# One program for a pooling block, an attention block and a mixture of experts: new starting stage, new opening of the experts, new ending

## What is computed

```python
def first_block(x, ...):
    for layer in range(2):
        h = rms_norm(x, mix_pre_g[layer])
        if layer < 1:
            m = pool_mixer(h, pool_w[layer], pool_scale[layer])
        else:
            m = stick_breaking_attention(h @ w_q, k, v) @ w_o
        x = x + rms_norm(m, mix_post_g[layer])
        h = rms_norm(x, mlp_pre_g[layer])
        x = x + rms_norm(square(relu(h @ w_up)) @ w_down, mlp_post_g[layer])
...
def pool_mixer(h, w_grp, scale):      # windows 2, 4, 8, 16, one for each 256 channels
    ...                               # mean of the last w tokens, minus the token itself
    y = einsum('bsgc,gcd->bsgd', y, w_grp).reshape(B, S, D)
    return y * scale
...
def hierarchical_moe(h, ...):         # 4 groups of 8 experts, two experts for a token
    act = silu(h @ w_gate) * (h @ w_up) * comb
    y = y + act @ w_down              # then h + y
```

## Time and profile before

| | us |
|---|---|
| median of three runs | 1147.08 |
| the profiled execution | 1151.92 |
| its span in the trace | 1150.1 |
| first product of the first up projection | 41.6 |
| first products of the experts (gather) | 703.0 |
| last chunk there, its products begin | 1138.1 |

### The profile page before, as it was taken

How to read it: one execution, slowest core, us unless ns; L and a number is a source line. 1 busy time by engine, 2 the same in 40 slices (tenths; PEclk the granted TensorE clock), 3 DMA queues, 4 the chain that set the end, 5 groups by cost and what they waited for, 6 DMA issues and landing times.

```text
span 1150.1 us, 14626 instructions
## 1 busy us (share of the span) xinstructions
PE 953.5 (83%) x5897; PEld 713.3 (62%) x5897; DVE 483.6 (42%) x798; ACT 384.0 (33%) x687; POOL 1.9 (0%) x7
## 2 busy tenths in 40 slices
PE   5899999999998999999799888967675656566666
PEld 4789998879866998998688776424141423232231
DVE  3655565665456566556766763220101010101010
ACT  3554554564475455455555532100000000000000
POOL 0000000000000000000000000000000000000000
PEclk9899999999999999999899998988887878888879
DMA  9545455544305354545440688999999999999995
GB/s 355 207 156 211 152 213 182 183 165 157 137 2 178 132 198 172 213 151 215 147 142 6 249 325 329 427 427 427 428 429 428 427 429 429 429 429 427 427 422 234
DMA packets 62738, 310.44 MB, mean 270 GB/s; under 512 B 2529, under 2 KB 3553, under 8 KB 52321
## 3 DMA queue, kind: packets, MB, share of 16 engines
q1 hardware_dynamic: 62256, 308.17, 67.7%
q0 software_dynamic: 432, 1.57, 0.5%
HBM read 308.68 MB, written 1.05 MB: 269 GB/s over the span
## 4 chain that ended last, share of the span: by engine, by line
PE 69%; DMA 17%; DVE 8%; ACT 4%; issue 2%; SPq 1%; DVEq 0%
DMA ring<-in_w_exp_down 17%; PE ps L636 15%; PE ps L637 14%; PE ps L638 14%; PE ps L1073 6%; PE ps L1117 6%; PE ps L1057 5%; PE ps L1129 3%; DVE w_lo L1655 1%; PE ps L827 1%; SPq L595 1%; DVE hT_lo L1636 1%; ACT w_hi L1238 1%; PE ps L701 1%; ACT hT_hi L1208 1%
## 5 line engine op out<-in xcount | busy, mean ns | idle before, releaser
L1642 DVE TENSOR_TENSOR w_lo<-ring,w_hi 128x1024 fp32r<-128x1024 f32 x158 | 190.7, 1223 | 84.7 <-ACT w_hi L1223 84.7
L1223 ACT ACTIVATE w_hi<-ring 128x1024 fp32r<-128x1024 f32 x158 | 164.5, 1054 | 88.3 <-PE ps L638 82.2
L1073 PE MATMUL ps<-ring,x 128*32 128x512 f32 x992 | 128.8, 677 | 78.6 <-DMA ring<-in_w_exp_up 67.3
L636 PE MATMUL ps<-hT_hi,w_hi 128*128 128x256 f32 x656 | 188.0, 287 | 4.5 <-DVE hT_lo L1636 2.7
L637 PE MATMUL ps<-hT_lo,w_hi 128*128 128x256 f32 x656 | 186.8, 285 | 0.0
L638 PE MATMUL ps<-hT_hi,w_lo 128*128 128x256 f32 x656 | 186.8, 285 | 0.0
L1073 PEld LDWEIGHTS ps<-ring,x 128*32 128x32 f32 x992 | 37.7, 123 | 163.4 <-issue 160.7
L636 PEld LDWEIGHTS ps<-hT_hi,w_hi 128*128 128x128 f32 x656 | 127.1, 194 | 6.4 <-issue 5.0
L637 PEld LDWEIGHTS ps<-hT_lo,w_hi 128*128 128x128 f32 x656 | 127.2, 194 | 0.5
L638 PEld LDWEIGHTS ps<-hT_hi,w_lo 128*128 128x128 f32 x656 | 127.0, 194 | 0.0
L1117 PE MATMUL ps<-ring,moe 128*32 128x512 f32 x512 | 69.3, 701 | 56.4 <-DMA ring<-in_w_exp_down 55.0
(11 more groups left out here) (280 smaller groups left out, 1176.6 us busy)
## 6 DMA issues: line engine op xcount, KB each, us to landing
ring<-in_w_exp_down SPq DMA_DIRECT2D x32, 2048.0 KB, 19.7
ring<-in_w_exp_gate SPq DMA_DIRECT2D x31, 2048.0 KB, 19.4
ring<-in_w_exp_up SPq DMA_DIRECT2D x31, 2048.0 KB, 20.4
ring<-in_w_up SPq DMA_DIRECT2D x16, 2048.0 KB, 8.1
ring<-in_w_down SPq DMA_DIRECT2D x16, 2048.0 KB, 7.8
ring<-in_w_in SPq DMA_DIRECT2D x6, 2048.0 KB, 8.5
ring<-in_w_kv SPq DMA_DIRECT2D x4, 2048.0 KB, 10.3
ring<-in_w_q SPq DMA_DIRECT2D x2, 2048.0 KB, 9.7
```

The lines of the kernel that those rows point to most:

```text
L636: mm(out, a_hi, b_hi, start=start, stop=False, skip_group_check=True)
L1073: last = mm(wk(side)[q, :], xgT[:, k, q], w4[:, j, k % 2, :] if opening else w[j][:, k, :], start=(k == 0), stop=(k == KD - 1))
L1223: fn(parts(n if edge else None, f)[0].rearrange("p (k w) -> p k w", k=KD), src, ACT.Copy).then_inc(hi_ready, 1)
L1642: ve.tensor_tensor(lo, src, hi.bitcast(F32), ALU.subtract).then_inc(lo_ready, 1)
```

## The change

**Start.** `x` comes in two transfers with a semaphore each, and the norm, `h`, the pooling and the mixer's own norm are done for one half at a time. `poolm` holds only what isn't zero: 144 columns (BAND) for half 0, 128 for half 1. `packed` is in two: its first 56 columns early, the rest now behind `consts`. The transfers keep their order. PE first writes zeros into banks 4 to 7 (16 products), and the pooling adds to them. `scale_row` is multiplied into `pool_w` on DVE (`pool_scaled`), in two parts, instead of into the result. ACT takes pooled groups 0 to 5, DVE 6 and 7; line 711's successor waits group by group. The squares are taken from `acc` in halves of 512 channels by ACT while DVE multiplies the other half by `row`. The splits of the first `w_up` chunk stand behind the mixer: quarter 0 between the token halves, 1 to 3 behind both. `keep_busy` is 8 ahead of the second half's transposes instead of 14 ahead of the first's.

```diff
+            for s in range(TT):
+                sp.dma_start(x[:, s, :], a["x"][0, s * P:(s + 1) * P, :]).then_inc(x_loaded[s], 16)
+            sp.dma_start(kbuf[:, 0:pool_ends[-1]], a["poolm"]).then_inc(poolm_loaded, 16)
+            sp.dma_start(packed[:, 0:S_QKG], a["packed"][:, 0:S_QKG]).then_inc(packed_loaded, 16)
...
-            sp.dma_start(row[:, :], a["mix_post_g"][0].partition_broadcast(P)).then_inc(scale_loaded, 16)
+            sp.dma_start(row[:, :], a["mix_post_g"][0].partition_broadcast(P)).then_inc(gain_loaded, 16)
+            load(N_MLP[0], kd_rows(a["w_up"][0])[:, :, 0:COLS], KD, COLS)
+            sp.dma_start(consts[:, :], a["consts"]).then_inc(consts_loaded, 16)
+            sp.dma_start(packed[:, S_QKG:], a["packed"][:, S_QKG:]).then_inc(packed_rest_loaded, 16)
...
+            pe.wait_ge(zero_ready, 1)
+            for b in range(4):
+                keep_busy(4 + b, 4)
             pe.wait_ge(poolm_loaded, 16)
+            pe.wait_ge(h_ready, 1)
+            for k in range(KD):
+                mm(wk(k // 2)[:, (k % 2) * T:(k % 2) * T + BAND], h[:, 0, k * P:(k + 1) * P], poolm[0][:, k // 2, :],
+                   start=False, stop=False, skip_group_check=True)
...
                 for g in range(4):
+                    if s == 0:
+                        pe.wait_ge(pool_scaled, g // 2 + 1)
+                        pe.wait_ge(yT_lo, g + 1) if g < 3 else pe.wait_ge(yT_hi, 1)
...
-                    if s == layer:
-                        keep_busy(7, (14, 10)[layer])
+                    if s == 1:
+                        keep_busy(7, (8, 10)[layer])
...
+            mix_half(0)
+            root(0, mix_ms, 1, mix_r0)
+            mix_half(1)
+            act.wait_ge(consts_loaded, 16)
+            root(1, mix_ms, 2, mix_r0)
             take_half(0, 0, 0, 0)
-            for f in (2, 3):
+            split(1, 0, quarter(1, 0))
+            take_half(0, 1, 2, 0)
+            for f in (1, 2, 3):
                 split(1, f, quarter(1, f))
```

and on DVE:

```diff
+            for part in range(2):
+                w = slot(N_POOL)[:, 1024 * part:1024 * part + 1024].rearrange("p (g c d) -> p g c d", g=2, c=2)
+                scales = scale_row[:, 512 * part:512 * part + 512].rearrange("p (g d) -> p g d", g=2)
+                ve.tensor_tensor(w, w, scales.unsqueeze(2).to_broadcast([P, 2, 2, 256]), ALU.mult).then_inc(pool_scaled, 1)
...
+            def mix_half(s):
+
+                dve.wait_ge(quarters_used, 2 * s + 2)
+                for half in (1, 0):
+                    if half == 0:
+                        dve.wait_ge(mix_squares, 2 * s + 1)
+                    c = slice(half * COLS, (half + 1) * COLS)
+                    ve.tensor_tensor(mg[:, s, c], acc[:, s, c], row[:, c], ALU.mult).then_inc(mix_gained, 1)
...
             for s in range(TT):
+                mix_half(s)
+                mix_add(s)
```

```diff
+            seed(0, 0)
+            turn_half(x, 1, x_ready, 10, 6)
             router(0)
-            turn_half(x, 1, x_ready, 10, 6)
             router(1)
...
+            seed(0, 1)
+            keep_busy(7, 7)
+
             pe.wait_ge(ind_ready, 1)
...
+                    for pair in range(4):
+                        gather(pair)
+                        if pair < 2:
+                            seed(1, pair)
+                        elif pair == 3:
+                            turn_weights()
+                        pe.wait_ge((xg_lo, xg_hi)[pair // 2], pair % 2 + 1)
+                        project_slots(0, (2 * pair, 2 * pair + 1), None)
```

```diff
+                            if closing and c == CPB - 1:
+
+                                sp.dma_start(dst[:, :, 0:COLS], src[:, :, 0:COLS]).then_inc(loaded, 16)
+                                sp.dma_start(dst[:, :, COLS:], src[:, :, COLS:]).then_inc(tail_loaded, 16)
+                                continue
...
+                        if closing and f == 3 and half == 1:
+                            pe.wait_ge(tail_loaded, 16)
...
+                        if closing:
+                            last.then_inc(moe_done, 1)
...
+            for half in range(2):
+                act.wait_ge(moe_done, 2 * half + 1)
+                leave(half)
             with act.If(n_most > SLOTS):
```

235 lines of the change are left out of this document (126 added, 109 removed).

## The result

| | us |
|---|---|
| the changed kernel, median of four runs | 1136.18 (1135.7 to 1138.89) |
| the kernel before, median of four runs beside it | 1147.15 |
| ratio | 0.990, 95% interval 0.9886 to 0.9914 |
| the profiled execution of the changed kernel, and its span | 1138.89, 1137.1 |
| the forecast | 1128.4 (1123.5 to 1133.5) |

Faster by 11 us, and 7.8 us short of the forecast; two more jobs with the unedited changed kernel gave 1134.82 and 1134.85, 13.0 under the kernel before of the same jobs. The direction and most mechanisms were right, the size and the range were not.

A forecast was written before the change was run, and what follows sets the result against it. TensorE's order of work was taken to bound the kernel up to the router, then the stream of experts' weights. Start -15.1, opening -0.7 and ending -2.9 sum to -18.7: 1147.08 to 1128.4 us, range 1123.5 to 1133.5.

The forecast's parts named there:

- start and both blocks: Start up to the experts: -15.1 us from an earlier up projection and full clock; feed-forward 1, attention and second block unchanged.
- opening: Opening of the experts: fewer seeds ahead of the gather free chunk 0 earlier; -0.7 us, with low clock in the gather +1.5.
- tail: Ending: half the last products remain and only the last store's issue follows its copy; -2.9 us, -3.6 if the branch is free.
- The start's step of 12.1 us: First mixer done by halves: TensorE starts the up projection at 29.5 instead of 41.63, 12.1 us earlier.
- Quarter 1's thin cover: First up projection: the split of quarter 1 comes at 31.7, TensorE wants it at 32.4; cover 0.7 us thin.
- The clock term of 3.0 us: First up projection: the clock stays up where 6.13 us ran at 0.50; 3.0 us more, bounds 0 and 3.1.
- rival 1: Clock falls in the start or one more place later: 6.13 us at half speed stay, +3.0, 1131.4; chance 0.15.
- Falls further on: Short clock falls behind the start may land elsewhere when everything comes earlier; taken as 0, with 3 us either way.
- a second hole: Opening: the stream gets a second hole of 2.4 us ahead of load 13, which can only flow at 725.2.
- rival 4: Opening: copies and waits of the pairs run the stream dry longer, low clock in the gather; +2.2, 1130.6; chance 0.09.
- a second transfer's fixed time: Ending, last chunk in two loads: no gap between transfers taken; about 2.0 us each in series would leave -0.9, whole 1130.4.
- rivals 1 to 4: Beside rivals 1 and 4: late loads (`scale_row` at 13.4), 1130.8, chance 0.09; fewer clock falls further on, 1125.4, chance 0.10.

The follow-up runs named there:

- consts_first: Changed kernel with the 532 KB of consts issued ahead of the pooling matrix's weights, scale row and first up chunk instead of behind them; 1136.92 us.
- before_again: The kernel before, unedited, profiled a second time; 1148.67 us, ratio 1.0006.
- before_busy: The kernel before with 5 more zero products ahead of the first transposes and 10 more behind them; 1147.94 us, ratio 1.0000.
- end: The kernel before with only the ending's part of the change (last chunk in two loads, quarters copied and stored singly); 1145.84 us, ratio 0.9983.
- after_third: The changed kernel, unedited, measured again in a third job; 1134.85 us, ratio 0.9879.
- start: The kernel before with only the start part of the change (loads and first mixer); 1137.2 us, ratio 0.9924.
- kb18: The changed kernel with 18 instead of 7 zero products between the second seed and the counting of the tokens; 1133.53 us, ratio 0.9875.
- kb18_again: The changed kernel with 18 instead of 7 zero products ahead of the counting, a second time; 1133.76 us, ratio 0.9866.
- after_again: The changed kernel, unedited, measured again beside its own variants; 1134.82 us, ratio 0.9879.
- nopass: The changed kernel without its overflow passes, which these inputs never take, on all engines; 1133.79 us, ratio 0.987.
- one_load: The changed kernel with the last chunk loaded in one again, the rest of the ending kept; 1138.52 us, ratio 0.9919.

## Why the prediction was wrong where it was

From the second profile of the kernel before (span 1146.5) to the mean of the three of the unedited changed kernel (1135.3), by the parts of the table:

| part | forecast | measured |
|---|---|---|
| start and both blocks | -15.1 | -9.9 |
| opening | -0.7 | +0.8 |
| stream | 0 | -0.1 |
| tail | -2.9 | -1.9 |
| sum | -18.7 | -11.2 |

**The start's step of 12.1 us was right.** The first up product stands at 29.69, forecast 29.5; against the two profiles of before that is 11.94 and 11.60. The path is the one described, gated by `scale_row` (consts_first moved both by 1.2). `scale_row` landed 1.0 later than taken (12.04), and most of it was made up in the mixer norm and behind it: `x` of half 0 was added at 21.18, as against 20.6, half 1 at 25.2 as against 24.9. Quarter 1's thin cover did not open; PE is busy through both stretches above.

**The clock term of 3.0 us was the first error.** In the changed kernel the clock was 1.00, as forecast; but in before_again it was too, with the same 2.7 us of idle ahead. The step failed in its premise: a row of one profiled execution was taken as the kernel's. There was a sign of it in the table of times, 1151.92 for the profiled execution against runs of 1146.9 to 1147.2, and the prediction read it only as an offset to subtract ("as the median lies 4.8 under that execution"). It is the same 4 us: what made that execution long was what the change was to take away. before_busy bears it out, 0.0 gained with the clock held up. By the Trainium skill ("TensorE: Matmul & The Clock Gate", Part 4) transposes don't count as activity for the clock, which gave rival 1; no fall follows the transposes in any of 16 profiles with the new start, nor in before_again, end and before_busy with the old one. The one fall is in the first profile.

**Falls further on were priced at 0 with 3 either way.** The changed kernel had two near 214 and 225 us in all three of its profiles. Same stretches, same work, after_third and `start` (positions agree to 0.1 us there):

```profile
214.00:218.50 4.50, 4.50 (x14) 3.54 (x14) 4.39 (x11) 3.16 (x9) 0.20 (x1) 0.62 0.02 4
...
225.00:229.00 4.00, 4.00 (x12) 3.14 (x11) 2.21 (x10) 3.12 (x10) 0.00 (x0) 0.57 0.81 312
```

```profile
214.00:218.50 4.50, 3.70 (x17) 2.72 (x15) 4.40 (x10) 2.75 (x7) 0.53 (x1) 1.00 0.02 4
...
225.00:229.00 4.00, 4.00 (x18) 3.00 (x16) 2.66 (x9) 3.38 (x8) 0.00 (x0) 1.00 0.56 214
```

The seven profiles with both falls (two of them with a third near 290) have 190 MB left at 668.7 on average, the six with none before 300 us at 666.7: 1.9 us. kb18 lacks them and kb18_again has them, with the same code. Why one execution falls and another doesn't wasn't found, so whether the change makes these falls likelier stays open; one of four profiles with the start of before had them, as against seven of sixteen.

**The opening failed at the clock.** The step took the gather's start, counted back from 703.04, as the one thing that removing seeds moves, and put the low clock aside as a bound of +1.5. It is in ten of ten profiles with seven zero products: TensorE is idle for 2.18 us behind them, where four seeds stood before. Measured +0.8 against -0.7. The rest of the step was right: with 18 zero products the opening is 0.9 shorter than before (58.0 against 58.9), chunk 0 comes free earlier (load 10 is issued 4.9 us behind the first gather product in kb18_again, 7.3 before), and a second hole opens ahead of load 13, which SP shows as four issues from 703.52 on that take 11.92 us in the changed kernel (four of 8.91 before). This is rival 4 with its price of +2.2 over the forecast, measured +1.5; it had 0.09.

**The ending was nearly right by the sum of two errors.** At full clock the tail is 17.4 and 17.5 in after_third and after_again against 19.9 and 20.4: -2.7, forecast -2.9. Without TensorE's transfer of instructions it would be 15.7 (nopass), so the hidden half of the products and the single stores are worth 4.4, more than the 3.6 given for a free branch; and the branch, priced at 0.7 for what it costs its own engine, costs 1.7 to 2.0 through the DMA queue. (The sum for the last copy gives 1143.4, where the prediction writes 1143.5.) The prediction took over the 2.5 us from the last issue to the end of the earlier trace rows unchanged. That profile has the same 16 KB, but from 1145.04 to 1146.30, ahead of the last store's issue at 1147.2; the single stores come early enough to meet it. Where the last products meet a low clock, 1.4 to 3.3 us are lost. The same products at full clock, of after_again:

```profile
1124.07:1128.78 4.71, 4.69 (x16) 1.59 (x16) 1.38 (x2) 1.19 (x2) 0.00 (x0) 1.00 0.16 57
```

The first profile of the changed kernel had a clock of 0.73 there and 6.36 us; after_third is like after_again. That the split doesn't cost a second transfer's fixed time was right (one_load). By the rule of the Trainium skill that the prediction weighed, 2.0 us for each transfer, the chunk in two would have landed 2.0 later; it did by 0.1 to 0.25. (The section named there is on transfers that GpSimd issues; those of the last chunk are SP's.)

Together: 3.0 for a clock that needed no help, 0.5 for 12.1 against the 11.6 of the second profile, 1.9 for the falls at 214 and 225, 1.5 for the opening, and 1.0 in the tail (one low stretch in three profiles) make 7.9, for the 7.5 between -18.7 and -11.2. In the medians the gap is 7.8, 6.4 and 6.5. The range was too narrow for another reason too: it let rivals 1 to 4 happen one at a time, and the clock had more than one of them at once.

The version to take from here is kb18, 1133.5 and 1133.8, not resolved from the changed kernel by its times, but better by 1.7 us in its stage in each profile. A further 1.7 to 2.0 us lie in TensorE's branch by the profiles (1.0 by the medians of nopass and after_again, not resolved); a form that keeps the overflow passes and lets that branch come earlier was not tried.

## What to carry to other kernels

If the profiled execution is over its own median by more than the other runs scatter, a second profile of the kernel before comes first: a gain read from a low-clock stretch counts only if that stretch is in both. Who takes filler work out from ahead of a wait should look at what the engine does in that time and put zero products in its place, but only where no real work can be ready (18 ahead of the counting gained 1.7 us in the stage, 16 ahead of the last chunk lost 1.8). Behind the last instruction of an engine there is still its branch, whose load of instructions shares the DMA engines with the last store.

## What the runs showed of the hardware that I had not expected

- The low-clock stretches of one and the same program differ from execution to execution: the kernel before had 0.50 at 41 us in one profile and 1.00 in the next, with 2.71 and 2.73 us of idle time ahead; the changed kernel's last products took 6.4 us in one and 4.7 in two. Medians of the same kernel in three jobs lay 1.4 us apart.
- A branch over a long body on TensorE brings a load of 16 KB of instructions, 0.9 to 1.4 us long, and nine packets of the last store run behind it, the last of them 1.7 us after all others (after_again).
- The last MBs of the stream come slower than the rest: with 2.1 MB left, 4.9 us at the rate of the stream, the last byte took 7.1 to 8.5 us in all 20 profiles.
- The stream of 166 MB took 388.3 to 388.6 us in 19 of 20 profiles, whatever stood ahead of it.
